# Turning attention and recurrence operands with VectorE's 32x32 blocks and a DRAM scratch instead of on TensorE, in a one-layer hybrid block

## The reference, cut to what matters

```
h = rmsnorm(x, g_mix); z = h @ w_in                  # 2048 x 14848 columns
q_r, f_r, i_r, og_r, q_a, k_a, v_a, gate_a, gate_b = split_columns(z)
o_a = hgrn2_mixer(q_r, f_r, i_r, og_r, ...)          # 16 heads of 128, chunks of 64 positions
o_b = swa_sink_attention(q_a, k_a, v_a, sinks, ...)  # 32 query heads of 64, 4 key heads, band of 2 chunks
merged = concat([sigmoid(gate_a) * o_a, sigmoid(gate_b) * o_b])
x = x + merged @ w_out
x = x + square(relu(rmsnorm(x, g_mlp) @ w_up)) @ w_down
x = x + sigmoid(x @ w_ple_gate) * (p @ w_ple_proj)
return rmsnorm(x, g_final)
```

## Time and profile before

| | |
|---|---|
| median of the 3 runs | 1712.78 us |
| the profiled execution's own time | 1712.3 us |
| its span | 1710.6 us |
| TensorE busy | 1696.8 us, 99% |
| VectorE busy | 1102.8 us, 64% |
| ScalarE busy | 924.0 us, 54% |
| DMA moved | 315.32 MB, 184 GB/s |

### The profile page before, as it was taken

How to read it: one execution, slowest core, us unless ns; L and a number is a source line. 1 busy time by engine, 2 the same in 40 slices (tenths; PEclk the granted TensorE clock), 3 DMA queues, 4 the chain that set the end, 5 groups by cost and what they waited for, 6 DMA issues and landing times.

```text
span 1710.6 us, 22406 instructions
## 1 busy us (share of the span) xinstructions
PE 1696.8 (99%) x8697; PEld 1419.3 (83%) x8697; DVE 1102.8 (64%) x1405; ACT 924.0 (54%) x1227; POOL 20.1 (1%) x72
## 2 busy tenths in 40 slices
PE   9999999999999999999999999999999999999997
PEld 7887888888888888888888888888888888888886
DVE  6767857875668766687685565656565656566565
ACT  6566656555565555655545544544454545454454
POOL 4000000000000000000000000000000000000000
PEclk9999999999999999999999999999999999999999
DMA  7755565556655566555556565656566666665553
GB/s 229 213 175 173 174 178 166 179 176 179 186 175 177 173 182 186 176 170 174 183 180 208 182 200 179 203 178 203 183 199 185 197 186 196 184 199 188 180 189 131
DMA packets 163293, 315.32 MB, mean 184 GB/s; under 512 B 10161, under 2 KB 10482, under 8 KB 163058
## 3 DMA queue, kind: packets, MB, share of 16 engines
q1 hardware_dynamic: 162016, 312.01, 59.2%
q10 hardware_dynamic: 1170, 1.87, 0.3%
HBM read 311.74 MB, written 2.10 MB: 183 GB/s over the span
## 4 chain that ended last, share of the span: by engine, by line
PE 96%; POOL 1%; DVE 1%; ACT 1%; issue 0%; DMA 0%; ACTq 0%; DVEq 0%
PE acc L679 21%; PE acc L680 21%; PE acc L685 21%; PE acc L695 6%; PE turn L695 6%; PE turn L679 3%; PE turn L685 3%; PE turn L680 3%; PE turn L702 3%; PE acc L702 3%; PE turn L724 2%; PE turn L756 0%; PE turn L780 0%; PE turn L829 0%; PE turn L768 0%
## 5 line engine op out<-in xcount | busy, mean ns | idle before, releaser
L1350 DVE TENSOR_TENSOR w_lo<-w_raw,w_hi 128x1024 fp32r<-128x1024 f32 x588 | 720.0, 1224 | 560.7 <-ACT w_hi L990 557.1
L990 ACT ACTIVATE w_hi<-w_raw 128x1024 fp32r<-128x1024 f32 x588 | 622.5, 1059 | 695.1 <-PE acc L685 438.0
L679 PE MATMUL acc<-w_hi,hT 128*128 128x512 f32 x1104 | 434.8, 394 | 1.1 <-ACT w_hi L990 1.1
L680 PE MATMUL acc<-w_hi,hT 128*128 128x512 f32 x1104 | 430.2, 390 | 0.0
L685 PE MATMUL acc<-w_lo,hT 128*128 128x512 f32 x1104 | 295.4, 389 | 0.0
L679 PEld LDWEIGHTS acc<-w_hi,hT 128*128 128x128 f32 x1104 | 207.3, 188 | 45.4 <-ACT w_hi L990 2.6
L685 PEld LDWEIGHTS acc<-w_lo,hT 128*128 128x128 f32 x1104 | 207.3, 188 | 43.5
L680 PEld LDWEIGHTS acc<-w_hi,hT 128*128 128x128 f32 x1104 | 207.4, 188 | 41.6
L679 PE MATMUL acc<-w_hi,mT_hi 128*128 128x512 f32 x416 | 164.4, 395 | 0.0
L680 PE MATMUL acc<-w_hi,mT_lo 128*128 128x512 f32 x416 | 162.2, 390 | 0.0
L695 PE MATMUL acc<-hT,w_hi 128*128 128x512 f32 x448 | 138.9, 391 | 0.0
(11 more groups left out here) (249 smaller groups left out, 1558.1 us busy)
## 6 DMA issues: line engine op xcount, KB each, us to landing
w_raw<-in_w_in_dram SPq DMA_DIRECT2D x232, 512.0 KB, 3.7
w_raw<-in_w_up_dram SPq DMA_DIRECT2D x128, 512.0 KB, 3.9
w_raw<-in_w_down_dram SPq DMA_DIRECT2D x128, 512.0 KB, 4.4
w_raw<-in_w_out_dram SPq DMA_DIRECT2D x64, 512.0 KB, 3.7
w_raw<-in_w_ple_gate_dram SPq DMA_DIRECT2D x32, 512.0 KB, 3.8
x_sb<-in_x_dram SPq DMA_DIRECT2D x8, 256.0 KB, 7.4
w_raw<-in_w_ple_proj_dram SPq DMA_DIRECT2D x4, 512.0 KB, 4.2
out_dram<-x_sb SPq DMA_DIRECT2D x6, 256.0 KB, 3.1
```

The source lines that it names most:

```text
L679: pe.matmul(a, hi[:, k, t, :], w_hi[:, s, kk, :], start=first and kk == 0, stop=False)
L680: pe.matmul(a, lo[:, k, t, :], w_hi[:, s, kk, :], start=False, stop=False)
L990: act.activation(w_hi[:, n % W_SLOTS], w_raw[:, n % RAW_SLOTS], ACT.Copy)\
L1350: dve.tensor_tensor(w_lo[:, n % W_SLOTS], w_raw[:, n % RAW_SLOTS], w_hi[:, n % W_SLOTS].bitcast(F32), ALU.subtract).then_inc(w_lo_ready, 1)
```

## The change

The 192 transposes on TensorE go. In their place, for each of six operands of a round (`TURNED` = qa, f, p0, q, gb, p1, where p0 and p1 are the softmax weights of the two tiles of positions): VectorE transposes 32x32 blocks in place of the position with two instructions of 128x512 into a buffer (`blocks`, the tiles eg and eg2, which hold the output gates later in the round); SyncE stores the buffer to a scratch in DRAM with four DMAs of 32 partitions each, which put block row b of column block c where block (c, b) belongs; ScalarE loads the scratch back with one DMA of 128 rows of 4 KB; and the users read the turned tile in SBUF instead of the bank. Stores stand eight chunks behind the blocks in SyncE's stream (`TO_STORE`; that stream runs four chunks ahead), loads six chunks behind in ScalarE's (`TO_LOAD`), and the users move: SCORES from (4, 16) to (7, 19), the values from (16, 28) to (22, 35), the end of the attention from 31 to 37, F_TURN, Q_TURN, DECAY and KE_TURN as shown below.

```
-        SCORES, PV1, ATT_END = (4, 16), 28, 31
+        SCORES, VALUES, ATT_END = (7, 19), (22, 35), 37
-        F_TURN, Q_TURN, DECAY, KE_TURN = (9, 26), (17, 28), (20, 35), (25, 40)
+        F_TURN, Q_TURN, DECAY, KE_TURN = (16, 33), (24, 36), (27, 39), (32, 44)
+        TURN_AT = {"qa": -4, "f": 9, "p0": 13, "q": 17, "gb": 20, "p1": 25}
+        TO_STORE, TO_LOAD = (8, 8), 6
@@ SyncE
+            def store_turned(kind, j, half):
+                i = turn_number(kind, j)
+                sp.wait_ge(blocks_turned, 2 * (i + 1))
+                rows_ = turned_rows[i].rearrange("(c i) b x -> b i c x", c=4)
+                for b in (2 * half, 2 * half + 1):
+                    sp.dma_start(rows_[b], flat_rows(blocks[i % 2])[32 * b:32 * b + 32]).then_inc(blocks_stored[i % 2], 16)
@@ TensorE, steps
-                    if a == -3:
-                        for t in range(TT):
-                            pe.wait_ge(qa_rotated, 2 * j + t + 1)
-                            turn(("qaT", j, t), lambda i: zb[:, t, i * P:(i + 1) * P])
...
-                            if t == 1:
-                                weighted_values(j, 0)
-                        for g in range(2):
-                            if a == SCORES[t] + 7 + 2 * g:
-                                weights_turn(j, t, g)
-                    if a == PV1:
-                        weighted_values(j, 1)
+                        if a == VALUES[t]:
+                            weighted_values(j, t)
...
-                        if h == F_TURN[hp]:
-                            pe.wait_ge(f_out, 2 * (j + 1))
-                            head_turn("fT", j, hp, za)
@@ TensorE, weighted_values
-                pe.wait_ge(pT_out, 2 * (2 * j + t + 1))
+                pe.wait_ge(pT_landed, 16 * (2 * j + t + 1))
...
-                                       pT[:, hh, :, qs], start=True, stop=True, skip_group_check=True)
+                        mm = pe.matmul(out_[:, :, bs], vv[:, v, j, :], pT[:, bs, hh].rearrange("p b k c -> p k b c"),
+                                       start=True, stop=True, skip_group_check=True)
@@ ScalarE
+            def load_turned(kind, j):
+                i = turn_number(kind, j)
...
+                act.wait_ge(blocks_stored[i % 2], 64 * (i // 2 + 1))
...
+                act.dma_start(to, turned_rows[i][:]).then_inc(landed, 16)
...
-                            act.wait_ge(full(("fT", j, hp)), nth(("fT", j, hp)))
-                            act.activation(hf[:], bank(("fT", j, hp))[:], ACT.Exp, scale=-1.0).then_inc(f_exp, 1)
+                            act.wait_ge(fT_landed, 16 * (j + 1))
+                            act.activation(by_blocks(hf), turned_block(flat_rows(za), 4 * hp, 4), ACT.Exp, scale=-1.0)\
+                               .then_inc(f_exp, 1)
@@ VectorE
+            def turn_blocks(kind, j):
+                i = turn_number(kind, j)
+                if i >= 2:
+                    dve.wait_ge(blocks_stored[i % 2], 64 * (i // 2))
...
+                for part in range(2):
+                    if kind in ("p0", "p1"):
+                        dve.transpose(to[:, 4 * part:4 * part + 4], pr[:, :, part, 0:P].rearrange("p k (b c) -> p k b c", b=4))\
+                           .then_inc(blocks_turned, 1)
+                    else:
+                        src = {"qa": zb, "f": za, "q": zb, "gb": sgb}[kind]
+                        dve.transpose(to.rearrange("p (k t) b c -> p t k b c", t=TT)[:, part],
+                                      src[:, part].rearrange("p (k b c) -> p k b c", k=4, b=4)).then_inc(blocks_turned, 1)
...
-                                dve.tensor_copy(pT[:, :, 2 * g:2 * g + 2, :],
-                                                bank(name)[:].rearrange("p (h k c) -> p h k c", h=2, k=2))\
-                                   .then_inc(pT_out, 1)
```

More of the change, by code:

```diff
@@ L272, in program @@
         kTd_out = sem("kTd_out")
+        blocks_turned = sem("blocks_turned")
+        blocks_stored = [sem(f"blocks_stored{i}") for i in range(2)]
+        qaT_landed = sem("qaT_landed")
         qaT_out = sem("qaT_out")
+        fT_landed = sem("fT_landed")
+        qT_landed = sem("qT_landed")
+        gbT_landed = sem("gbT_landed")
+        pT_landed = sem("pT_landed")
         nm_ready = sem("nm_ready")
         pr_ready = sem("pr_ready")
-        pT_out = sem("pT_out")
         pv_out = sem("pv_out")
@@ L327, in program, with turn_number, turned_block, flat_rows @@
         out_stored = sem("out_stored")
+        TURNED = ("qa", "f", "p0", "q", "gb", "p1")
+        turned_rows = [nc.dram_tensor(f"turned_rows{i}", [P, 4, 256], F32, kind="Internal")
+                       for i in range(NG * len(TURNED))]
+        blocks = (eg, eg2)
+        def turn_number(kind, j):
+            return len(TURNED) * j + TURNED.index(kind)
+        def turned_block(tile, m0, nm):
+            return tile.rearrange("p b (m c) -> p m b c", c=32)[:, m0:m0 + nm]
+        def flat_rows(tile):
+            return tile[:].rearrange("p t (b x) -> p (t b) x", b=2)
         def count(value, r=0, per=0):
@@ L524, in parts_of, with by_blocks, by_tile @@
             return ((slice(0, CHUNK), CHUNK), (slice(CHUNK, P), P)) if t == 0 else ((slice(0, P), P),)
+        def by_blocks(tile):
+            return tile[:].rearrange("p (m b c) -> p m b c", m=4, b=4)
+        def by_tile(tile, t):
+            return turned_block(flat_rows(tile), 0, 8).rearrange("p (k t) b c -> p t k b c", t=TT)[:, t]
         def four(ap):
@@ L578, in _ @@
                     load_x(slot[0])
+                for j in range(NG):
+                    for kind in TURNED:
+                        for half in range(2):
+                            if slot[0] == A0[j] + TURN_AT[kind] + TO_STORE[half]:
+                                store_turned(kind, j, half)
             for r in range(ROUNDS):
@@ L1080, in steps @@
                         z_out("qa", j, za, qa_out)
-                    if a == -2:
+                    for kind in TURNED:
+                        if a == TURN_AT[kind] + TO_LOAD:
+                            load_turned(kind, j)
+                    if a == 5:
+                        act.wait_ge(qaT_landed, 16 * (j + 1))
+                        if j:
+                            for hh in range(2):
+                                act.wait_ge(full(("score", j - 1, 1, hh)), nth(("score", j - 1, 1, hh)))
                         for t in range(TT):
-                            act.wait_ge(full(("qaT", j, t)), nth(("qaT", j, t)))
-                            act.activation(qT[:, :, t, :], four(bank(("qaT", j, t))[:]), ACT.Copy)\
+                            act.activation(qT[:, :, t, :].rearrange("p k (b c) -> p k b c", b=4), by_tile(zb, t), ACT.Copy)\
                                .then_inc(qaT_out, 1)
```

87 lines of the change are left out of this document (39 added, 48 removed).

## The result

| | median | ratio to the kernel before on the same chip, 95% interval |
|---|---|---|
| changed kernel | 1693.05 us (1692.94 to 1693.21, 4 runs) | 0.9885 (0.9868 to 0.9902) |
| before, beside it | 1712.74 us (4 runs) | |

The kernel became 19.7 us faster, where 1692 us and a gain of 21.3 were predicted. The profiled execution took 1692.94 us, its span is 1691.0 us against 1710.6.

A forecast was written before the change was run, and what follows sets the result against it. TensorE's instruction stream was taken as the bound: 5.32 us net a round over four rounds, 21.3 us, off 1712.3 gives 1691.0, plus 0.5 for the median, written as 1692; the 8-in-10 range was 1689 to 1703 us.

The forecast's parts named there:

- TensorE's stream is the time: TensorE is busy 1696.8 of 1710.6 us; whatever leaves its stream comes off the time; sum holding within 2 us: 0.68.
- 5.44 us a round leave: Transpose groups leaving TensorE each round: doubles 1.80, singles 2.82, shared places 0.82; net 5.32 after one start-up returns.
- The values' start-up, taken as 0.12: First tile's values, now alone after chunk 22 on TensorE, pay one more start-up of 0.12 us a round.
- the rival of leads that run out: Stalls on VectorE and ScalarE line up in each round, losing 2 to 3 us each: 1702 us, chance 0.15.
- Values no slower: TensorE's products reading pT in 32-column runs stay at 1.01 us a tile; rival of up to 8.1 us slower: 0.06.
- VectorE at 0.69: Each 128x512 block transpose on VectorE takes 0.69 us; 48 make 33 us, 22 more net of the dropped copies.
- that end: Upper bound of 1.22 us a transpose: VectorE's densest stretch has 3.2 us more than it holds, under 6.8.
- The lead: ScalarE's rounded weights are ready usually 6.8 us, at least 4.0, before TensorE reads them; shorter hold-ups cost nothing.
- 3.2 to 5 us of engines a turn: Price of storing and loading back one turned operand, 512 KB each way, on the DMA engines; 4.4 us are free.
- 5.8 us a turn: DMA price from which time is lost, 4.4 + 6.8 / 5; the DMA-bound rival: 1775 us, chance 0.07.
- Less the lead of 6.8: In the DMA-bound rival, 27.5 us short a round less the 6.8 us lead leaves 20.7 lost a round.
- issuing had been called cheap: Four stores take 1.8 us of SyncE; ScalarE's 24 loads add 11 us in all, under half a microsecond in any chunk.

The follow-up runs named there:

- experiment 2: Changed kernel with 192 identity transposes put back on TensorE, 24 in a row ahead of each tile's scores: 1713.61 us, ratio 1.0007.
- experiment 6: Changed kernel with the second recurrence one chunk later, KE_TURN (32, 44) to (32, 45): 1692.12 us, ratio 0.9880.
- experiment 3: Changed kernel with every block transpose made twice, 48 more on VectorE: 1702.43 us, ratio 0.9943.
- experiment 1: Changed kernel without the scratch stores and loads; blocks still turned, users read the unturned tile, weights' blocks go straight to pT: 1692.54 us, ratio 0.9883.
- experiment 5: Changed kernel with twice the transfers, every store made twice and one copy within DRAM behind each load: 1714.81 us, ratio 1.0015.
- experiment 4: Changed kernel with every store made three times and two copies within DRAM behind each load: 1758.19 us, ratio 1.0265.
- experiments 9 and 10: Changed kernel with only the stores made twice: 1698.80 us, ratio 0.9918; with only one DRAM copy behind each load: 1695.61 us, ratio 0.9902.
- experiment 7: On top of experiment 6, the values moved beside the recurrence, to (32, 45), attention's end to 46, p1's load three chunks later: 1714.98 us, ratio 1.0015.

## Why the prediction was right, and where it was off

- **TensorE's stream is the time.** Right, and shown from both sides: 192 turns out gave 19.7 us, 192 turns back cost 20.6 (experiment 2), without anyone waiting for them.
- **5.44 us a round leave.** Chunk by chunk the two traces differ by 4.44 us in round 0 and by 5.28, 5.18 and 5.16 in the others, 20.06 in all, where 4 x 5.32 = 21.3 was the sum. Two terms, the next two, hold the missing 1.2.
- **The values' start-up, taken as 0.12, is 0.26.** With the scores alone two chunks take 105.33 - 98.59 = 6.74 us, with the values alone 148.67 - 141.99 = 6.68; less 5.44 for two plain chunks each, that is 2.54. Before, with both in one place, the two chunks around them took 8.06 us (126.35 to 134.41 in the rows below), of which 0.35 are the four turns of q: less 5.44, 2.27. So standing apart costs 0.27 here and 0.26 in the mean, four times 0.14 more than assumed, 0.56 us. The error: a start-up was counted behind the small products only, and the change of kind ahead of them costs as well (the scores start 1.00 us behind the last w_lo products, 100.40 to 101.40, where a plain chunk's next product starts 0.91 behind).

```profile
126.35 0.39 PE L679 MATMUL acc<-w_hi,hT 128*128 128x512 f32 x1
...
134.06 0.60 PE L724 MATMUL turn<-ident,zb 128*128 128x128 f32 x4
134.41 0.48 PE L679 MATMUL acc<-w_hi,hT 128*128 128x512 f32 x1
```

- **Round 0 lost 0.7 more.** Its second recurrence stood at the end of VectorE's fullest stretch, and waited 0.46 us for `ke` with a slow start behind it: that chunk grew by 2.27 us where it grew by 1.55 in the other rounds. Experiment 6 takes the wait away and gets 0.9 back. This is the rival of leads that run out, at 0.7 us instead of 10.
- **Values no slower.** 1.01 us a tile before and after. Right.
- **VectorE at 0.69.** 690 to 691 ns, busy time up by 20.3 us where 22 was the sum. Right, and it mattered more than the text allowed: with 1.22 VectorE would have got 25 us more (48 x 0.53), near the 33 (48 x 0.69) of experiment 3, which lost 9.4. The prediction had called that end harmless, with a slip in it: 38.60 + 6 x 1.22 - 1.4 is 44.5 against 41.8, so 2.7 us too much and not 3.2.
- **The lead.** The prediction read it from ScalarE's roundings alone. For w_hi the 4.0 us was nearly right (one chunk later, rounded by 188.16 and read at 191.82, it was 3.7 before; the least after is 4.0). The shorter lead is that of w_lo, on VectorE, which got the new work: 3.5 us before (made at 187.42, first read at 190.91), and after the change, from VectorE's and TensorE's rows around step 44 of round 0:

```profile
204.53 1.22 DVE L1381 TENSOR_TENSOR w_lo<-w_raw,w_hi 128x1024 fp32r<-128x1024 f32 x1
...
207.84 1.07 PE L724 MATMUL acc<-w_lo,hT 128*128 128x512 f32 x4
```

  w_lo is made at 205.75 and first read at 207.84, 2.1 us later, because VectorE has the decays and, in round 0, the bounds and sums of the output gates ahead of it. In rounds 1 to 3 the shortest are 2.4 to 3.0 us, at h = 32 (in round 2 also 2.8 at 44). The sum came out because this lead was not used up (but for the 0.46 us of `ke`), not because 6.8 us stood behind it.
- **DMA.** 3.2 to 5 us of engines a turn were taken, 2.3 measured, and experiment 1 bounds the cost of all of it at 0.5 us. Of the threshold the runs show the opposite: 5.8 us a turn was to be harmless, and at 5.4 the whole gain was gone (experiment 5). "Less the lead of 6.8" failed: with 2.1 in its place the same working gives (5.4 - 4.4) x 5 - 2.1 = 2.9 a round, 12 us, still short of 21.8, and for experiment 4 it gives 76 us where 65 were measured. The form of the working fails too. It lets a turn cost something only above the 4.4 us that are free; by the queues' shares experiments 9 and 10 are at 4.1 and 3.7 us a turn, and lost 5.8 and 2.6 us. That SyncE's eight issues stand ahead of the weights, 4.1 us, and that loads and blocks wait for all the stores, is in none of its terms; issuing had been called cheap. The landing of pT's loads, 5.4 us, is just not under the 5.4 that the prediction asked for, and cost nothing. On the split of a landing, the Trainium skill (DMA: Bandwidth & Descriptors, Anatomy of one DMA) gives about 2 us of fixed cost, mostly the receipt of the write, measured for DMAs that GpSimd issues; those here are issued by SyncE and ScalarE. The trace agrees in kind: stores and load land in 4.0 and 4.9 us and occupy the engines for 2.3 in all. It does not show the 2 us themselves.
- **Not placed:** the chunks account for 20.06 us, and the spans differ by 19.6. Of the rest, TensorE's first product starts 0.14 us later (9.78 instead of 9.64), and the chunk 61 behind H0 of round 3 is 0.16 longer; why was not found.
- **Slips without weight.** The earlier trace rows leave out the longest wait, 1.8 us for `ident`, which is the same before and after. The four rounds end with chunk 280, not 264; the steps within a round are as given.

## What to carry to other kernels

When one engine's instruction stream is the time, price an instruction by how far it moves the next piece of steady work, count a start-up on each side of a group that is left alone, and multiply; that gave this result within 1.6 us of 21.3. Do not judge the engine that receives the work by its share, but by the least lead of what it makes, in the place where its own late work piles up: 48 more instructions on VectorE cost 9.4 us at 68% busy. And price a mishap by what follows it: a wait of 3 us on TensorE cost 5.7, since the clock fell, and two delays of 5.8 and 2.6 us cost 21.8 together, most of it at a chunk whose lead was already short.

## What the hardware showed that was not expected

- After a wait of 3.0 us TensorE ran at a granted clock of 0.50 (1.2 GHz) until some 6 us later (experiment 7). Shorter waits did it too, and not each time: two of 0.90 and 1.11 us, 2.3 us apart, were followed by a window at 0.69, much the same pairs in the two rounds before left the clock at 1.00 (experiment 3); a wait of 2.16 us for pT, which ended at 315.11, was followed by 0.50 over 317 to 320 (experiment 5). 24 transposes in a row, 2.71 us, left it at 1.00 (experiment 2).
- A block transpose of 128x512 in float32 takes 691 ns on VectorE, as long as a copy from PSUM of that size.
- SyncE spends 0.5 us on issuing a 128 KB store (four take 2.00). On ScalarE the issue of a 512 KB load takes 0.3 us (0.33 at 169.08), and that of a copy within DRAM behind a load took 0.47 us in one place and 1.66 in another (experiment 5, 770.72 and 307.73).
